# Routing stage and expert stage of a MoE decoder step: sums ahead of the transposed copies, the first two search steps moved into the routing stage, and the shared down pieces spread over four steps

## The reference, cut to what matters

```
x = x + (mix @ w_out)
h = rms_norm(x, norm_ffn_w)
score = sigmoid(h @ w_router); idx = top_k(score + router_bias, 8)
g = 2.5 * score[idx] / sum(score[idx])
tokens sorted by expert, in padded blocks; for each block with its expert e:
    a = silu(h[tb] @ w_gate_e[e]) * (h[tb] @ w_up_e[e])
    acc[tb] += (a @ w_down_e[e]) * g
shared = (silu(h @ w_gate_s) * (h @ w_up_s)) @ w_down_s
x = x + acc + shared
```

## Time and profile before

| | us |
|---|---|
| median of the runs (lowest, highest) | 1536.1 (1534.09, 1537.1) |
| the profiled execution | 1531.07 |
| its span | 1529.4 |
| PE busy | 1367.2 (89%) |
| DVE busy | 614.0 (40%) |
| ACT, POOL busy | 345.9 (23%), 245.9 (16%) |
| DMA over the span | 424.08 MB, mean 277 GB/s |

### The profile page before, as it was taken

One profiled execution on the slowest core, in us unless ns is written; L12 is line 12 of the kernel. 1 busy time (PEld: TensorE's weight loads), 2 busy tenths in 40 slices (PEclk: granted clock), 3 DMA queues, 4 the chain that ended last, 5 costly groups with the idle time before them and its releaser, 6 DMA issues. The chain is left out here.

```text
span 1529.4 us, 30195 instructions
## 1 busy us (share of the span) xinstructions
PE 1367.2 (89%) x9894; PEld 724.9 (47%) x9895; DVE 614.0 (40%) x1813; ACT 345.9 (23%) x938; POOL 245.9 (16%) x291
## 2 busy tenths in 40 slices
PE   6999899999999998898969887779999999999892
PEld 2445566566667776444633222223444443333330
DVE  1524156676576665434633222222333333322233
ACT  1202235444434444300101111111111111111110
POOL 1000110005273320000001111111222222212120
PEclk9999889999999999999889988889999999999996
DMA  8312299999989999750087999999876999999976
GB/s 308 68 28 50 84 319 295 340 371 312 330 290 315 332 344 373 252 201 28 8 349 271 378 382 376 375 374 371 296 227 191 306 314 310 382 358 367 367 247 204
DMA packets 160681, 424.08 MB, mean 277 GB/s; under 512 B 48225, under 2 KB 51842, under 8 KB 134402
## 3 DMA queue, kind: packets, MB, share of 16 engines
q1 hardware_dynamic: 142928, 381.30, 68.4%
q0 software_dynamic: 14400, 38.82, 10.6%
q10 hardware_dynamic: 3250, 2.65, 0.5%
HBM read 395.25 MB, written 41.06 MB: 285 GB/s over the span
## 5 line engine op out<-in xcount | busy, mean ns | idle before, releaser
L2559 PE MATMUL ps_gu<-ring,mixT 128*32 128x512 f32 (+2 forms) x1664 | 364.6, 633 | 54.5 <-SPq L2317 53.6
L2559 PEld LDWEIGHTS ps_gu<-ring,mixT 128*32 128x32 f32 (+2 forms) x1664 | 125.0, 140 | 289.5 <-issue 253.6
L2578 PE MATMUL ps_y<-w_dn,aT_e 128*32 128x512 f32 (+2 forms) x832 | 175.9, 598 | 4.4 <-DVE aT_e L2473 2.4
L1509 PE MATMUL ps_kT<-ident,ring 128*128 128x128 f32 x1024 | 141.8, 281 | 10.2 <-DVE ring L1132 5.7
L1509 PEld LDWEIGHTS ps_kT<-ident,ring 128*128 128x128 f32 x1024 | 114.4, 144 | 68.4 <-ACT ring L967 34.7
L2471 DVE TENSOR_TENSOR act_in<-sil,ps_gu 128x256 f32<-128x256 f32 x48 | 20.2, 421 | 289.8 <-ACT sil L2391 289.8
L2343 POOL DMA_INDIRECT kT<-h_dram,idx x50 | 51.9, 1037 | 504.1 <-DVE idx L2432 504.1
L1132 DVE COPY ring<-ps_kT 128x512 f32<-128x512 f32 x128 | 88.3, 689 | 80.5 <-PE ps_kT L1509 78.2
L2391 ACT ACTIVATE sil<-ps_gu 128x256 f32<-128x256 f32 x48 | 18.4, 383 | 392.0 <-PE ps_gu L2559 392.0
L2347 POOL DMA_INDIRECT sums_dram<-qT,sidx x48 | 76.5, 1593 | 147.8 <-DVE qT L2481 143.9
L2578 PEld LDWEIGHTS ps_y<-w_dn,aT_e 128*32 128x32 f32 (+2 forms) x832 | 55.4, 132 | 93.4 <-issue 85.7
(11 more groups left out here) (525 smaller groups left out, 1687.9 us busy)
## 6 DMA issues: line engine op xcount, KB each, us to landing
ring<-in_cache_k SPq DMA_DIRECT2D x256, 256.0 KB
ring<-in_cache_v SPq DMA_DIRECT2D x256, 256.0 KB, 4.7
ring<-in_w_gate_e SPq DMA_DIRECT2D x64, 1024.0 KB
ring<-in_w_up_e SPq DMA_DIRECT2D x64, 1024.0 KB
w_dn<-in_w_down_e SPq DMA_DIRECT2D x64, 1024.0 KB
w_in<-in_w_in SPq DMA_DIRECT2D x8, 1028.0 KB, 15.7
sums_dram<-w_dn SPq DMA_DIRECT2D x1, 4608.0 KB, 22.2
ring<-in_w_out SPq DMA_DIRECT2D x2, 2048.0 KB, 14.1
```

The costliest lines, as they stand in the source:

```text
L1509: last = pe.transpose(ps_kT[:, j % 2, e * PAGE:(e + 1) * PAGE], k_places[n % RING][:, e * DA + j * P:e * DA + (j + 1) * P], m.ident[:, :])
L2559: last = pe.matmul(ps_gu[at, :].rearrange("p (g n) -> p g n", g=2), xgT[:, u, k, at], w_gu[:, place, :, k, :].rearrange("p s g n -> p (s g ...
L2578: last = pe.matmul(ps_y[at, n, :], aT[:, j, at], w_dn[:, place, j, n * 512:(n + 1) * 512].rearrange("p s n -> p (s n)"), start=(j == 0), s ...
```

## The change

- In the tile loop DVE takes the sums of tile t ahead of the copies to `hT` of tile t-1 (`to_hT`). PE takes the router's product of tile 3 ahead of the transposes of tile 4.
- ACT runs a one-column sigmoid after the last norm, so that its table is switched there.
- The gates and three columns of `pick` are formed right after the top 8, ahead of the wait for the ranks; the multiplication by 2.5 is merged into that by the reciprocal.
- `choices`, `select`, `find`, `indices` and the gathers of steps 0 and 1 stand in the routing stage: `find` for both inside the shared product (1, 0), ACT's `choices` ahead of its second SiLU.
- In the expert stage PE begins with the transposes of step 0. The nine shared pieces go two to each of steps 0, 1 and 2 and three to step 3; steps 2 and 3 are written out. `MIN_TWO` is 12 rather than 8 (at least three loops of twos).
- `biased` and `rest` move into an unused part of `uT`.

The diff, cut to its core:

```diff
-MIN_TWO = 2 * PAIRED
+MIN_TWO = 3 * PAIRED
...
@@ routing stage, POOL @@
                 pool.memset(m.xg, 0.0)
                 pool.drain()
+                last_token = pool.to_reg(T - 1)
+                pool.wait_ge(h_out[0], 16 * 3)
+                pool.wait_ge(h_out[1], 16 * 2)
+                for u in range(2):
+                    pool.wait_ge(m.idx_done, u + 1)
+                    pool.sem_inc(first_turns, 1)
+                    gather(pool, m, u, last_token)
@@ routing stage, ACT @@
+                act.activation(inv[:, 1, 0:1], m.ones[:, 0:1], ACT.Sigmoid)
                 act.wait_ge(iota_done, 1)
                 act.wait_ge(r_mm, TT)
...
+                shared_silu(0)
+                act.wait_ge(tables_done, 1)
+                act.wait_ge(pick_done, 1)
+                choices(nc, act, m, 0)
+                choices(nc, act, m, 1)
+                shared_silu(1)
@@ routing stage, DVE, tile loop @@
                         last.then_inc(x1_done, 1)
+                    if t >= 1:
+                        to_hT(t - 1)
                     dve.wait_ge(ss_done, t + 1)
...
-                    for half in range(2):
-                        dve.wait_ge(tr_mm, 2 * t + half + 1)
-                        ...
+                to_hT(TT - 1)
@@ routing stage, DVE, after the top 8 @@
                 dve.tensor_reduce(gsum[:, 0, :], gate[:, :, :], AX.X, ALU.add)
+                dve.drain()
+                dve.reciprocal(gsum[:, 1, :], gsum[:, 0, :])
+                dve.drain()
+                dve.scalar_tensor_tensor(gate[:, :, :], gate[:, :, :], 2.5, over_experts(gsum[:, 1, :]), ALU.mult, ALU.mult)
+                dve.drain()
+                dve.tensor_copy(m.pick[:, :, :, 4], gate[:, :, :])
+                ...
+                dve.tensor_copy(m.pick[:, :, :, 6], part[:, :, :])
@@ routing stage, DVE, after the tables @@
                 dve.sem_inc(tables_done, 1)
+                ...
+                tt(m.pick[:, :, :, 3], over_experts(tok_f[:, 3, :]), tmp2.unsqueeze(1).to_broadcast((P, TT, NE)), ALU.subtract).then_inc(pick_done, 1)
+                dve.wait_ge(slots_done, 1)
+                dve.drain()
+                select(nc, dve, m, 0)
                 ts(m.free_tab[:, :], free_i[:, :], QUAD.bit_length() - 1, None, ALU.arith_shift_right)
...
+                indices(dve, m, ps[:, 7, 0:N_COL], 0, 1)
+                select(nc, dve, m, 1)
+                indices(dve, m, ps[:, 7, 0:N_COL], 1, 2)
@@ routing stage, PE @@
+                router(TT - 2)
                 transposes(TT - 1)
-                router(TT - 2)
                 router(TT - 1)
...
-                shared(1, 0, range(KD), 0)
+                shared(1, 0, range(KD // 2), 0)
+                find(pe, m, ps[:, 7, 0:N_COL], 0)
+                shared(1, 0, range(KD // 2, KD), 0)
+                find(pe, m, ps[:, 7, 0:N_COL], 1)
                 shared(1, 0, range(KD), 1)
@@ expert stage @@
-        BEFORE = 4
+        AT_STEP = (0, 2, 4, 7)
...
-                for u in range(2):
-                    select(u)
-                    indices(u, u + 1)
...
-                find(0)
-                find(1)
-                for c in range(BEFORE):
-                    shared(c)
                 transposes(0, 16, None)
...
-                step_of(0, 16, 0, 2, TWO[0], BEFORE)
-                step_of(1, 32, 1, 4, TWO[1], BEFORE + 3)
-                with pe.Fori(1, n_two) as i:
+                for step, piece in enumerate(AT_STEP):
+                    needed = registers(nc, ENG.PE, use_tab, step * 2, 1, 1, NE)[0] if step >= 2 else 2 * step + 2
+                    step_of(step, 16 * (step // 2 + step % 2 + 1), step % 2, needed, TWO[step % 2], piece)
+                with pe.Fori(2, n_two) as i:
```

More of the change, by code:

```diff
@@ L1957, in _, with to_hT @@
                 dve.wait_ge(x_again, 16 * TT)
+                def to_hT(t):
+                    n = rows(t)
+                    for half in range(2):
+                        dve.wait_ge(tr_mm, 2 * t + half + 1)
+                        c = m.col["norm_ffn"] + 4 * half
+                        w = m.columns[:, c:c + 4].unsqueeze(2).to_broadcast((P, 4, n))
+                        tt(hT[:, 4 * half:4 * half + 4, cols(t)], ps[:, half, :].rearrange("p (k n) -> p k n", n=P)[:, :, 0:n], w, ALU.mult).then_inc(hT_done, 1)
                 for t in range(TT):
@@ L2258, in experts @@
     sem = m.sem
-    BF = mybir.dt.bfloat16
     use_tab = m.use_tab[:, :, :].rearrange("o s c -> o (s c)")
@@ L2372, in _ @@
                 n_loops = loops(ENG.Activation)
-                def choices(n):
-                    experts_of = registers(nc, ENG.Activation, m.exp_tab, n * QUAD, QUAD, 0, NE - 1)
-                    if not isinstance(n, int) or n:
-                        act.wait_ge(idx_mm, n)
-                    for j in range(QUAD):
-                        last = act.copy(tg[:, :, j, :], m.pick[:, :, bass.ds(experts_of[j], 1), :].rearrange("p t e c -> p (t e) c"))
-                    last.then_inc(tg_done, 1)
                 def xT(b, tr):
@@ L2464, in step_of @@
                     step = i * 2 + u
-                    destinations(u, step, None if isinstance(i, int) else i * 16)
-                    select(step + 2)
-                    if sums_at is not None and sums_at > BEFORE + 2:
+                    first = isinstance(i, int) and i == 0
+                    destinations(u, step, None if first else i * 16)
+                    select(nc, dve, m, step + 2)
+                    if sums_at == AT_STEP[-1]:
                         shared_sum(sums_at - 1)
@@ L2478, in step_of @@
                     dve.wait_ge(dn_mm, i * 4 + (2 * u + 2))
-                    if not isinstance(i, int):
+                    if not first:
                         dve.wait_ge(scattered[u], i * 16)
@@ L2503, in _ @@
             def _(pe):
-                n_two, n_four = registers(nc, ENG.PE, m.loop_tab, 0, 2, 2, MAX_LOOPS)
+                n_two, n_four = registers(nc, ENG.PE, m.loop_tab, 0, 2, 3, MAX_LOOPS)
                 n_loops = loops(ENG.PE)
-                def find(n):
-                    pe.wait_ge(sel_done, n + 1)
-                    pe.wait_ge(tg_done, n + 1)
-                    if not isinstance(n, int) or n:
-                        pe.wait_ge(idx_done, n)
-                    for t in range(TT):
-                        for j in range(QUAD):
-                            at = slice(j * BLK, (j + 1) * BLK)
-                            last = pe.matmul(ps_idx[at, 0:N_COL], sel[0:rows(t), t, at], tg[0:rows(t), t, j, :],
-                                             start=(t == 0), stop=(t == TT - 1), tile_position=(0, j * BLK))
-                    last.then_inc(idx_mm, 1)
                 def transposes(b, got, taken, halves=(0, 1)):
@@ L2562, in step_of @@
                     last.then_inc(gu_mm, 1)
-                    find(step + 2)
+                    find(pe, m, ps_idx[:, 0:N_COL], step + 2)
                     transposes(1 - u, turn, step + 1, (0,))
```

144 lines of the change are left out of this document (73 added, 71 removed).

## The result

The changed kernel takes 1512.99 us, the median of 4 runs (1510.06 to 1515.21), against 1535.09 us of the kernel before (4 runs, 1527.54 to 1537.1): a ratio of 0.986, 95% interval 0.9831 to 0.9889. The forecast was 1516, range 1510 to 1522. The profiled execution took 1511.85 us and its span is 1510.1.

The account below looks back on a forecast made before the run. The prediction took the weight stream of the twos to set the pace: -10 (earlier first load) - 14.8 (DMA idle removed) + 5 (idle left) = -19.8 us, giving a median of 1516 us from 1536.1, range 1510 to 1522.

Parts of the forecast that it names:

- The bound: Expert stage: DMA, then PE, then DMA; an earlier weight stream of the twos moves everything behind it as much.
- D: Rival: twos not DMA-bound once earlier, or gain given back at the large experts; no change, 1536 us, chance 0.03.
- Tile loop: Routing tiles 2 to 4: PE's three waits for DVE's sums go, with late sums and slow records; -8.1 to -9.7 us.
- Gates ahead of the ranks: After the top 8: 4.7 us of gates into a 4.38 us wait, cost 0.4; slow ranks and shared products up to 3.
- Search inside: Routing stage: PE waits about 2.9 us at the first find; SP's load of expert 3 at 773.5 us, costing nothing.
- a rule against the change: PE's new waits at find, mask and barrier may be paid again in slow clock: plus 3 us, 1519.
- Step 0: First step of twos: starts at 780 instead of 803.45 us, product ends at 790 instead of 810.5, 3 us for slow clock.
- B: Rival: step 0's gathers land only when all four experts have, 12 + 2 us DMA idle; 1525 us, chance 0.15.
- the DMA idle time behind the first four experts: Weight stream: 5 us idle in place of 14.8, 2 ahead of expert 4 and 3 at later loads.
- Cover of the shared pieces: Steps 1 to 3: shared pieces hidden by the weights' arrival, with 3.5 us to spare at step 4.
- C: Rival: PE stays at 1.2 GHz through steps 0 to 3, 12.7 us longer a step; 1564 us, chance 0.04.
- A: Rival: new waits cost no clock, tables_done moves by 11, DMA idle falls to 2; -24, 1512 us, chance 0.2.

Follow-up runs that it names:

- Experiment 1: The kernel before with only the new tile loop and router order; 1521.26 us, 0.992 of the kernel before.
- experiment 7: The changed kernel with three unused 128x512 products ahead of PE's first find; 1504.87 us in one run.
- experiment 6: The kernel of experiment 5 with one shared piece ahead of PE's register loads, the other eight two to a step; 1504.26 us, 0.9803 of the kernel before.
- experiment 4: The changed kernel with both finds one shared product later in PE's list; 1507.87 us, 0.9845 of the kernel before.
- 10: The changed kernel with one shared piece ahead of PE's register loads, the other eight two to a step; 1508.74 us, 0.9826 of the kernel before.
- 2: The changed kernel with the old tile loop and router order put back; 1519.85 us, 0.9911 of the kernel before.
- experiment 5: The kernel of experiment 4 with SP reading tables first and requesting expert 4 before waiting for experts 2 and 3; 1506.95 us, 0.9822 of the kernel before.
- experiment 8: The changed kernel run and profiled again, unchanged; 1507.79 us, 0.9828 of the kernel before.
- Experiment 3: The changed kernel with four shared pieces ahead of step 0 again, the other five in steps 0 and 1; 1520.65 us, 0.9914 of the kernel before.

## Why the prediction was right

**The bound.** It rested on the weight stream setting the pace of the twos. PE's waits there still end by SP's report alone (ten, 39.6 us, against eleven, 44.3, in the earlier trace rows), step 4 among them, and the large experts take 201.6 of 204 us. What was gained before step 4 arrived at the end: 15.4 us of the 17.6 in the first pair of profiles (857.9 against 842.5 from the transposes to the end), 20.7 against 20.6 over all. D is refuted.

**Tile loop.** Forecast 8.1 to 9.7 plus 1.74 for the scores, cut to 10 for the first load; measured 11.65. The upper ends of the terms were right: all three waits, the slow half of tile 4, the 2.0 of the late sums and the wait for scores went. Experiment 1 shows that it is this edit alone. The delayed copies do hold PE, for 1.95 us at the router's product of tile 3, but not DVE, on which the first load hangs. The first load was to move to 753.5 to 756.5; it moved to 749.16, 3.85 us of which lie ahead of the stage's transposes and are the execution's own. Without them it is 753.0, still just outside.

**Gates ahead of the ranks.** Forecast a cost of 0.4 and up to 3 more if the ranks ran at the slow clock. From the top 8 to DVE's copy of the ranks it is 8.52 before (745.50 - 736.98) and 8.87 after (730.27 - 721.40): 0.35, as forecast, and nothing of the 3. Up to the first load no more than 0.1 of it is left, 27.7 before (764.66 - 736.98) and 27.8 after (749.16 - 721.40).

**Search inside.** The wait was forecast at 2.9 and is 2.93. That it would also cost clock stood in the forecast as a rule against the change (+3, 1519), since the trace of before was of two minds. It did: 0.50 granted from 753 to 759, 6.59 for 3.65, and experiment 7 gets the 2.9 back by filling the wait. The rule of the Trainium skill (TensorE: Matmul & The Clock Gate, "The HAM clock gate"), that the slow clock is the default and activity releases it, agrees with that row and with the piece of experiment 6; which short waits are paid for does not follow from it, and three of the four waits of 2.7 us at tile 2 in the kernel before were not. The price cost little in the end, since the first three experts were still landing and SP's own list held the next request (below): experiment 7, without it, has step 4 at 182.4.

**Step 0.** Forecast from 780 to 790, measured from 778.28 to 787.64 (9.36 long, of which 2.3 for the clock; forecast 3), which is 782.1 to 791.5 with the 3.85 added back. PE stood 4.81 between the stages. The gather was issued at 754.97, landed 8.5 us later, and nobody waited for it: B is refuted, in the way that the row of 10.10 us had suggested.

**The mis-sized term** is the DMA idle time behind the first four experts: 5 forecast, 7.7 measured. 6.4 of it lie ahead of expert 4, where the forecast had 2. It took the end of step 0's product, 35.3 us behind the first load (790 - 754.7), as what SP's request for expert 4 waits for. The product ended 38.5 behind, mainly by the search's clock price, but that is not the reason: SP waited for it 0.4 us (waits of SP from 780 to 790):

```profile
SPq L1781 <- PE ps_gu L2584: 0.4, 1, 0.4
```

What held SP until then was its own list, which the forecast had left out: the fourth expert's landing, and then two table reads, the first at 784.6, 35.4 behind the first load. In experiments 4, 10, 7 and 2 the product ended 32.3, 34.1, 35.4 and 36.6 behind the first load, and expert 4 was asked for 38.6, 38.3, 38.1 and 38.2 behind it. So with step 0 as early as forecast 5 to 6 us would have been idle there all the same. A late step 0 costs behind that request, where down of expert 4 waits for it until 794.87: over the 100 us behind the first load the DMA was idle 8.7 us in the changed kernel, 6.6 in experiment 7, 5.6 in experiment 4 and 2.6 in experiment 5 (stretches of 3 us, summed).

**The sum** comes out near by two errors of opposite sign: -11.65 - 6.0 = -17.6 for this pair of profiles against -10 - 9.8 = -19.8, and -20.6 over all profiles. That the first median, 1512.99, lies in the range of 1510 to 1522 and the second, 1507.79 (experiment 8), below it is within what two sets of runs of one kernel differ by.

**Cover of the shared pieces.** Steps 1 to 3 start at 796.68, 812.80 and 832.60, 16.1 and 19.8 apart (forecast 15.8 and 18.9), at a granted clock of 1.00; C is refuted. Step 3 waited 0.83 and step 4 2.64 for weights, together the forecast 3.5 us of cover. Experiment 3 shows what spreading them was worth: 6.0.

**A, the rival with more gain,** failed in its cause (the waits did cost clock), though its time, 1512, is nearer to the first median than the forecast. Its first number, 11 at the load, was right and its second, 2 us of idle, wrong.

## What to carry to other kernels

When a ring of buffers is full, the stream's next hole is set by whichever comes last: the first consumer's end, the landing of the last buffer, or the rest of the issuing engine's own list. Count all three; here the list hid the gain of an earlier consumer at the next request (38.1 to 38.7 us behind the first load in five kernels whose product ended 32.3 to 38.5 behind it), and only the requests behind it profited. A short wait on TensorE can cost twice, once as waiting and again as slow products behind it; useful work put ahead of it or into the engine's register loads (experiments 4, 6 and 10) avoids the second price in the profiles, though none of these kernels is shown to be faster than the changed one. And compare stretches from a landmark inside the profile over several executions: here one pair of profiles understated the gain by 3 us.

## What the hardware showed beyond the expectation

The same wait does not always cost the same. In four profiles of the kernel before, a wait of 2.70 or 2.71 us at tile 2 was followed by a product of 3.67 three times and of 5.13 once; 2.55 us at the last tile by one of 5.07 to 6.54; the first product of the routing stage, always behind 2.99 us of PE's sequencer, took 3.67, 5.37 or 6.59 in different executions and kernels; and the 2.93 us at the search were followed by 5.29 to 6.69. In the kernel before the instructions ahead of each wait were the same each time, so such waits add to the scatter: two of them make 2.4 of the 7.1 us (95.6 against 93.2 at the first load) by which one profile of the kernel before needed more to step 4 than another. Whether the changed kernel's times scatter less isn't shown.
